# Where the outer products of the sample states are formed: eight VectorE instructions, or ScalarE scalings and one VectorE add

## What is computed

```
f  = lb + (1 - lb) * sigmoid(rf)           # decay, per key dimension
k  = 1 - f
S' = f[:, None] * S + k[:, None] * i[None, :]     # new state, 128 keys x 128 values
o  = q @ S'
```

## Time and profile before

| | us |
|---|---|
| runs: median (lowest to highest of 3) | 1192.67 (1191.17 to 1195.02) |
| profiled execution: its own time | 1192.0 |
| its span, first to last instruction | 1189.9 |
| TensorE busy | 1167.1 (98%) |
| VectorE busy | 885.9 (74%) |
| ScalarE busy | 532.2 (45%) |
| GpSimd busy | 241.4 (20%) |

### The profile page before, as it was taken

One profiled execution on the slowest core, in us unless ns is written; L12 is line 12 of the kernel. 1 busy time (PEld: TensorE's weight loads), 2 busy tenths in 40 slices (PEclk: granted clock), 3 DMA queues, 4 the chain that ended last, 5 costly groups with the idle time before them and its releaser, 6 DMA issues.

```text
span 1189.9 us, 23028 instructions
## 1 busy us (share of the span) xinstructions
PE 1167.1 (98%) x8965; PEld 1148.6 (97%) x8965; DVE 885.9 (74%) x1506; ACT 532.2 (45%) x1189; POOL 241.4 (20%) x190
## 2 busy tenths in 40 slices
PE   9999999999999999999999999999999999999997
PEld 9899989899998999999999999999999999999996
DVE  4988587675769756799777887997897565577676
ACT  5766656755242654565222322322222244455542
POOL 1000020101020000000133256764664020000011
PEclk9999999999999999999999999999999999999999
DMA  9431101006484334252554657667765386775466
GB/s 304 120 94 37 36 19 38 19 2 106 58 104 111 91 135 133 74 151 67 154 161 154 195 171 252 224 217 231 243 225 167 112 267 183 222 239 184 143 150 115
DMA packets 174011, 169.77 MB, mean 143 GB/s; under 512 B 23144, under 2 KB 126328, under 8 KB 173376
## 3 DMA queue, kind: packets, MB, share of 16 engines
q1 hardware_dynamic: 171728, 164.78, 47.3%
q0 software_dynamic: 2176, 3.52, 1.9%
HBM read 116.73 MB, written 52.58 MB: 142 GB/s over the span
## 4 chain that ended last, share of the span: by engine, by line
PE 79%; DVE 12%; ACT 4%; issue 3%; DMA 2%; SPq 0%; ACTq 0%; DVEq 0%
PE pair L1958 34%; PE pair L1998 19%; PE pair L1700 12%; PE pair L1917 7%; PE pair L1775 1%; PE pair L1829 1%; DMA mix<-x_cols_dram 1%; DVE ast L2332 1%; DVE hqk L2219 1%; DVE hqk L2214 1%; DVE w_lo L2427 1%; PE pair L1790 1%; PE pair L1814 1%; PE pair L1794 1%; DVE mix L2499 1%
## 5 line engine op out<-in xcount | busy, mean ns | idle before, releaser
L1958 PE MATMUL pair<-act_hi,w_hi 128*128 128x258 f32 x704 | 199.1, 283 | 1.1 <-DVE u_tmp L2577 1.1
L1958 PE MATMUL pair<-act_hi,w_lo 128*128 128x258 f32 x704 | 198.6, 282 | 0.0
L1958 PE MATMUL pair<-act_lo,w_hi 128*128 128x258 f32 x704 | 198.6, 282 | 0.0
L1998 PE MATMUL pair<-a_ring,w_hi 128*128 128x258 f32 x1056 | 191.6, 284 | 0.5 <-DVE mix L2637 0.4
L1700 PE MATMUL pair<-act_hi,w_hi 128*128 128x344 f32 x528 | 176.6, 334 | 0.9 <-DVE act_lo L2077 0.8
L1700 PE MATMUL pair<-act_hi,w_lo 128*128 128x344 f32 x528 | 168.6, 319 | 0.0
L1700 PE MATMUL pair<-act_lo,w_hi 128*128 128x344 f32 x528 | 168.4, 319 | 0.0
L1998 PEld LDWEIGHTS pair<-a_ring,w_hi 128*128 128x128 f32 x1056 | 163.1, 189 | 1.5 <-DVE mix L2637 0.8
L1197 ACT ACTIVATE w_hi<-rawx 128x512 fp32r<-128x512 f32 (+3 forms) x100 | 69.9, 699 | 199.7 <-PE pair L1958 79.4
L1958 PE MATMUL pair<-mix_r,w_hi 128*128 128x258 f32 x528 | 149.3, 283 | 0.0
L1958 PE MATMUL pair<-s_hi,w_hi 128*128 128x258 f32 x528 | 149.1, 282 | 0.0
(11 more groups left out here) (349 smaller groups left out, 2643.0 us busy)
## 6 DMA issues: line engine op xcount, KB each, us to landing
raw<-w_up_dram SPq DMA_DIRECT2D x26, 512.0 KB, 5.3
a_in<-h_sums SPq DMA_DIRECT2D x44, 258.0 KB, 3.1
rawx<-w_gate_dram SPq DMA_DIRECT2D x22, 512.0 KB, 5.2
w_quarter<-w_down_dram SPq DMA_DIRECT2D x44, 256.0 KB, 3.8
w_sums<-w_quarter SPq DMA_DIRECT2D x44, 256.0 KB, 4.7
rawx<-w_sums SPq DMA_DIRECT2D x44, 256.0 KB, 3.8
raw<-w_in_dram SPq DMA_DIRECT2D x18, 512.0 KB, 3.9
h_scratch<-mix SPq DMA_DIRECT2D x23, 258.0 KB, 2.2
```

The source lines that it names most:

```text
L1958: mm = pe.matmul(pair[psum_pair(n)][:, s, 0:QW], a[:, r, half + k, :], b, start=(k == 0 and i == 0), stop=(k == 3 and i == 2))
L1998: mm = pe.matmul(dpair(mt)[:, s, 0:a.shape[1]], b[:, cut], a, start=(m == 0 and n == 0), stop=(m == HALVES - 1 and n == 2))
```

## The change

The table gets two new steps, `r_keys` in ticks t+1 and t+2, in each of which ScalarE multiplies four of the eight spread rows in `ib` by the sample's key, in place (four instructions, 128x128). `r_outer` moves one tick on, to t+3, and is one VectorE instruction over the whole tile, `st = st + ib`. The semaphore that it waits for is raised by ScalarE. The wait for the keys moves to ScalarE. To free semaphores, three of the lower bound's become one with three values.

```diff
-            out += [(s, h) for s, v in (("r_scale", 0), ("r_outer", 2), ("r_o", 4)) if d == v]
+            out += [(s, h) for s, v in (("r_scale", 0), ("r_keys", 1), ("r_keys", 2), ("r_outer", 3), ("r_o", 4)) if d == v]
...
-                act.wait_ge(sem("lb_ready"), 1)
+                act.wait_ge(sem("lb_step"), 3)
...
-                act.wait_ge(sem("lb_in"), 1)
-                act.activation(lbt[:, 2:4, :], lbt[:, 0:2, :], ACT.Exp).then_inc(sem("lb_exp"), 1)
+                act.wait_ge(sem("lb_step"), 1)
+                act.activation(lbt[:, 2:4, :], lbt[:, 0:2, :], ACT.Exp).then_inc(sem("lb_step"), 1)
...
+                if step[0] == "r_keys":
+                    h = step[1]
+                    a = 4 * (tick - (SR0 + SRS * h) - 1)
+                    act.wait_ge(sem("s_ib"), 16 * (h + 1))
+                    act.wait_ge(sem("hk_prep"), 2 * h + 2)
+                    for b in range(a, a + 4):
+                        ins = act.activation(ib[:, b, :], ib[:, b, :], ACT.Copy, scale=k_s[:, h, b:b + 1])
+                    ins.then_inc(sem("ib_keys"), 1)
...
                 if step[0] == "r_outer":
                     h = step[1]
-                    dve.wait_ge(sem("s_ib"), 16 * (h + 1))
+                    dve.wait_ge(sem("ib_keys"), 2 * h + 2)
                     dve.wait_ge(sem("st_scaled"), h + 1)
-                    dve.wait_ge(sem("hk_prep"), 2 * h + 2)
-                    for b in range(DECB):
-                        ins = dve.scalar_tensor_tensor(out=st[:, b, :], in0=ib[:, b, :], scalar=k_s[:, h, b:b + 1], in1=st[:, b, :],
-                                                       op0=ALU.mult, op1=ALU.add)
-                    ins.then_inc(sem("s_state"), 1)
+                    dve.tensor_tensor(st[:], st[:], ib[:], ALU.add).then_inc(sem("s_state"), 1)
```

More of the change, by code:

```diff
@@ L2116, in lower_bound @@
             dve.tensor_tensor(lbt[:, 0, :], lbl[:, 0, :], lbt[:, 4, :], ALU.subtract)
-            dve.tensor_tensor(lbt[:, 1, :], lbl[:, 1, :], lbt[:, 4, :], ALU.subtract).then_inc(sem("lb_in"), 1)
-            dve.wait_ge(sem("lb_exp"), 1)
+            dve.tensor_tensor(lbt[:, 1, :], lbl[:, 1, :], lbt[:, 4, :], ALU.subtract).then_inc(sem("lb_step"), 1)
+            dve.wait_ge(sem("lb_step"), 2)
             then(dve.tensor_tensor(lbt[:, 5, :], lbt[:, 2, :], lbt[:, 3, :], ALU.add))
@@ L2122, in lower_bound @@
             then(dve.tensor_scalar(lbt[:, 5, :], lbt[:, 4, :], -0.5, 0.5, ALU.mult, ALU.add))
-            dve.tensor_tensor(lbt[:, 6, :], lbt[:, 4, :], lbt[:, 5, :], ALU.add).then_inc(sem("lb_ready"), 1)
+            dve.tensor_tensor(lbt[:, 6, :], lbt[:, 4, :], lbt[:, 5, :], ALU.add).then_inc(sem("lb_step"), 1)
         def rope(u):
```

## The result

| | before | the change |
|---|---|---|
| runs: median (lowest to highest) | 1193.35 (1191.17 to 1195.02, 4 runs) | 1208.89 (1208.49 to 1212.26, 4 runs) |
| profiled execution: its own time | 1192.0 | 1208.67 |
| its span | 1189.9 | 1206.8 |
| mean granted clock of TensorE | 0.998 | 0.990 |

The ratio on record is 1.0139, with a 95% interval of 1.0124 to 1.0155 (the two medians alone give 1.0130): slower, as forecast, but by 15.5 us between the medians and not by 10. The time lies above the forecast's range (1198 to 1206).

A forecast was written before the change was run, and what follows sets the result against it. TensorE, busy 98% of the span, was taken as the bound, losing time only where it waits. Delays of 2.85 + 3.1 + 4.3 = 10.25 us on 1192.0 gave 1202.25, forecast as 1202.5 us, range 1198 to 1206.

The forecast's parts named there:

- Head 0: At L1889, TensorE waits for the add, which stands behind VectorE's chain of eight states: +2.85 us.
- Head 1: Eight scalings in ScalarE's full run delay the keys 2.4 us; with the later add, L1889 starts +3.1 us late.
- Head 2: The 1.69 us wait ahead of L1829 goes, but the add behind the output gate delays L1889: +0.6 us.
- Head 3: Krow copies come late behind four scalings, then L1889 waits for the add: +4.3 us together with head 2.
- Sum: The added delays of all four heads at TensorE: 10.25 us on the profiled execution's 1192.0.
- The step that failed: TensorE's in-order queue: a wait at L1889 also holds the projection behind it, and the lost time stays lost.
- the late queue: Rival: SyncE holds loads until the state stores land, so TensorE waits for transfers; adds 1 to 3 us; chance 0.12.
- The test that was named: Sign expected afterwards: from the output projection on, everything shifted by one constant, near 10 us.
- Fewer instructions win: Rival: 28 fewer VectorE instructions and adds in time for L1889 remove the 1.69 us wait: 1191.0 us; chance 0.06.

The follow-up runs named there:

- the first version with the pauses filled: The change plus ten unused 128x128 products of ones on TensorE ahead of each of its four long waits; median 1206.91 us, profiled execution 1202.71.
- three heads, one tick back: Kernel before, with heads 0, 2 and 3 scaled on ScalarE in ticks t and t+1, add in t+2; head 1 unchanged; 1190.87 us, ratio 0.9988.
- one tick back: The change with all heads' scalings in ticks t and t+1 and the add in t+2; 1196.92 us, ratio 1.005 to the kernel before.
- the version with both changes: Kernel before, with scalings and earlier add on heads 0, 2, 3, and head 2's decay on ScalarE instead of GpSimd; 1190.38 us, ratio 0.9977.

## Why the prediction missed

**The mechanism of the pauses was right.** Each pause came at the instruction, behind the producer and for the reason that was forecast; the add is 1.22 us (1.63 once beside GpSimd), four scalings 1.27.

**Their sizes were nearly right, and in sum a little too high.**

- Head 0: +2.85 forecast, +2.60 measured. The chain of states ended at 324.14 and the add followed at once; the whole piece is as forecast.
- Head 1: keys +2.4 forecast, +2.30 measured. The further +0.7 of the add did not come: L1897 (352.76) has no pause. The add started at 350.42 and took 1.63, while TensorE was still at the diagonal, which had become 1.4 us longer by the half clock. A slower TensorE hid the late add; at full clock, in the profile of the first version with the pauses filled, the same products wait 0.53 us there.
- Head 2: +0.6 forecast, +0.99 measured. The pause of 1.69 us ahead of the level moved to L1897, as 2.19, and 1.17 us of another stayed at level 4.
- Head 3: +3.7 forecast (4.3 with head 2's 0.6), +2.67 measured. The wait that was forecast for the krow copies did not come, since TensorE itself arrived late. At full clock, in the same filled profile, it is there, 1.23 us long (the row below).
- Sum: 10.25 forecast, 8.56 measured. In that filled profile, at full clock and with the products of ones aboard, the span is 11.0 us above the kernel before: near the forecast, which had priced a full clock.

```profile
386.36 2.05 PE L1857 MATMUL pair<-irow,krow 128*128 128x128 f32 x16 [1.23 <-ACT krow L1197]
```

**The step that failed** is the one ahead of the sum: "when L1889 waits, the projection behind it waits too ... what is lost here stays lost", and with it the sum itself, in which every pause costs its own length. Nothing in it stands for products that run slower behind a pause. The measured term is 9.7 us on top of 8.6. (What follows the stretch is some 800 us, 390 to 1190, and not the 400 of the prediction; no term of the sum uses that figure.) None of the rivals had it either, and the late queue, which forecast a time above 1203.5, had another mechanism of which the trace shows nothing: no pause of TensorE in this stretch is ended by a transfer.

It could have been read in part. The trace of before has a granted clock in every window. It shows 0.50 from 1185 us to the end of the span at 1189.9, where TensorE is done, so the low level and its size were in sight; what was not there was a pause above 1.7 us in this stretch, and so no row for what one does.

**The test that was named** ("everything shifted by one constant, near 10 us") fails in a telling way: the shift is nearly constant behind the mixer (16.8 to 17.2 us), but it is 16.9 and not 10, and inside it, it grows also where TensorE does not wait, from 2.60 to 5.87 in the ledger between head 0 and the squares.

**Fewer instructions win** was given little and is true in a form that was not asked: with the add in time (three heads, one tick back) the kernel gains 0.12%, and 0.23% with the decay moved too. The rival's condition, an add that ends before TensorE's arrival, was stated rightly.

## What to carry over

A pause that a change brings to a TensorE that has been at work without a break is priced twice: its own length, and behind pauses of 2 us and more 1.4 to 5.1 us of products lost at half clock (behind 13 of the 14 such pauses that are listed here). Whether several short pauses are cheaper than one long one no run compares; behind short ones the clock fell in some executions only. A change that only moves work must be read for where it stands in each in-order queue: the same instructions cost +1.4% behind the chain of states and +0.4% ahead of it, and the exchange on three heads, a tick earlier and out of ScalarE's full run, gave -0.1%. Read the granted clock in windows of 1 us beside the waits before adding up a sum.

## What the hardware showed besides

**Half clock behind pauses.** The level is 0.50 of 2.4 GHz each time, and the stretches lasted 3 to 11 us (the longest, 344 to 354.5, behind the pause of 2.38 us in the kernel with the add ahead of the chain). Among pauses of 2.2 to 4.4 us one, of 2.79, had none behind it; among those under 1.9 us most had none, but one of 1.85, one of 0.90 and one of 1.01 did. The levels' pauses of 0.7 to 1.8 us were followed by one in several kernels, and in one the longest pause near was 0.46. Filling the pauses with idle products kept the clock at 1.00 in one profile and all but once in the other; the mean clocks of the executions without a trace, down to 0.993, show that it does not always. In the kernel before the mean clock lies between 0.994 and 0.998 from one execution to the next, and the time follows it: part of the spread between executions goes with this clock.

**GpSimd holds VectorE.** Beside GpSimd's decay of the states, a VectorE instruction with two inputs from SBUF ends only behind it. Rows of the kernel before, of GpSimd, VectorE and TensorE, from their timelines:

```profile
354.16 1.90 POOL L1129 TENSOR_TENSOR st<-st,f_s 128x1024 f32<-128x1024 f32 x1 [8.27 <-DMA st<-state_hgrn_dram]
```
```profile
354.73 1.60 DVE L2214 TENSOR_TENSOR hqk<-mix,hg 128x256 f32<-128x256 f32 x1
356.37 0.43 DVE L2214 TENSOR_TENSOR mix<-hqk,hg 128x256 f32<-128x256 f32 x1
```
```profile
358.15 1.13 PE L1829 MATMUL pair<-hqk,mix 128*128 128x128 f32 x8 [1.33 <-DVE hqk L2219]
```

L2214 takes 0.43 us by itself (the median of its 24) and 1.60 here; it ends at 356.33, GpSimd at 356.06. VectorE's next decay is late by the 1.17 us, and TensorE waits 1.33 for it. The Trainium skill (SBUF — State Buffer, SBUF: two separate sides) says that GpSimd and a VectorE instruction with two SBUF inputs take one pair of ports in turn, each for a whole instruction. The trace agrees, 1.17 us for this one, and 1.66 in the profile of one tick back (L2216, 2.18 instead of 0.52). In the version with both changes ScalarE does the same decay in 2.46 us, and VectorE's two instructions beside it (L2232 there) take 0.47 and 0.42.
